# Reordering VectorE's masked products in the RWKV stage of a diffusion block kernel

## The reference

```python
def rwkv7_scan(r, w, k, v, kk, a, S):
    """All inputs (B,H,L,N); S (B,H,Nv,Nk).
    S_t = S_{t-1} (diag(w_t) - kk_t^T (a_t * kk_t)) + v_t^T k_t ;  y_t = S_t r_t."""
    def step(S, inp):
        rt, wt, kt, vt, kkt, at = inp
        sa = jnp.einsum("bhvk,bhk->bhv", S, -kkt)
        S = S * wt[:, :, None, :] + sa[..., None] * (kkt * at)[:, :, None, :] + vt[..., None] * kt[:, :, None, :]
        return S, jnp.einsum("bhvk,bhk->bhv", S, rt)
    S, ys = lax.scan(step, S, xs)
    return jnp.moveaxis(ys, 0, 2), S

y_c, y_l = bidir_scan(rwkv7_scan, init, *scan_args(pc), *scan_args(pl))
out_l = rwkv_out(y_l, pl, kvec, lnx, w_o)       # ((layernorm(y) + bonus) * g) @ w_o
```

## Time and profile before

| | |
|---|---|
| time before, median of 3 runs | 3686.1 us (3682.07 to 3688.07) |
| profiled execution, its own time | 3686.1 us |
| its span | 3684.3 us |
| TensorE busy (matmul) | 3408.9 us, 93% of the span |
| VectorE / ScalarE / GpSimd busy | 922.6 / 616.0 / 225.5 us |
| mean granted TensorE clock | 0.944 |
| HBM read | 567.19 MB |

### The profile page before, as it was taken

The page is one execution under the profiler, slowest core; times in us unless marked ns, Lnnn a source line. Parts: engine busy times, 40 slices in busy tenths (PEclk is TensorE's granted clock), DMA queues, the critical chain, the costliest instruction groups (busy, mean ns, idle before and its releaser), DMA issues. The chain is left out here.

```text
span 3684.3 us, 58147 instructions
## 1 busy us (share of the span) xinstructions
PE 3408.9 (93%) x25914; PEld 2490.3 (68%) x25914; DVE 922.6 (25%) x2050; ACT 616.0 (17%) x1416; POOL 225.5 (6%) x198
## 2 busy tenths in 40 slices
PE   6999996899999999999998799999989788888998
PEld 3777774698779877986456654444464577777887
DVE  0200015200001000101504514341030455553461
ACT  1010012200000000001313420000020334342100
POOL 0000000000000000000002210000000131311000
PEclk8999997899999999998998889999979999998999
DMA  9567741177777777775100113333321100003340
GB/s 376 225 249 305 309 175 58 52 286 274 282 281 284 276 282 283 282 276 212 57 35 2 59 68 117 123 114 145 118 83 40 40 23 13 23 3 139 117 158 23
DMA packets 86284, 577.28 MB, mean 157 GB/s; under 512 B 9488, under 2 KB 13584, under 8 KB 18192
## 3 DMA queue, kind: packets, MB, share of 16 engines
q1 hardware_dynamic: 82576, 568.27, 41.3%
q10 hardware_dynamic: 3456, 5.24, 0.4%
HBM read 567.19 MB, written 6.29 MB: 156 GB/s over the span
## 5 line engine op out<-in xcount | busy, mean ns | idle before, releaser
L261 PE MATMUL ps<-H,ring 128*128 128x256 f32 (+1 forms) x3600 | 1057.4, 456 | 16.8 <-ACT H L528 8.9
L261 PEld LDWEIGHTS ps<-H,ring 128*128 128x128 f32 x3600 | 693.9, 194 | 385.6 <-issue 317.8
L1399 PEld LDWEIGHTS ps<-W,ring 128*128 128x128 f32 x5632 | 639.5, 192 | 7.6 <-issue 3.3
L1399 PE MATMUL ps<-W,ring 128*128 128x128 f32 x5632 | 640.6, 275 | 1.2 <-ACT W L1432 1.2
L261 PE MATMUL ps<-W,ring 128*128 128x256 f32 (+1 forms) x1488 | 466.9, 475 | 10.4 <-DVE W L2514 8.0
L261 PEld LDWEIGHTS ps<-W,ring 128*128 128x128 f32 x1488 | 283.1, 191 | 197.7 <-issue 171.6
L1419 PE MATMUL ps<-ring,W 128*128 128x512 f32 x704 | 304.6, 592 | 0.0
L1480 DVE TENSOR_TENSOR W<-ps,W 128x128 f32<-128x128 f32 x176 | 51.3, 291 | 871.3 <-PE ps L1399 871.3
L1419 PEld LDWEIGHTS ps<-ring,W 128*128 128x128 f32 x704 | 132.6, 190 | 161.2 <-issue 161.2
L1648 DVE SCALAR_TENSOR_TENSOR W<-ps,vec,W 128x189 f32<-128x189 f32 (+3 forms) x396 | 173.3, 438 | 14.0
L3035 POOL TENSOR_TENSOR ring<-ring 128x512 f32<-128x512 f32 x96 | 124.5, 1313 | 528.3 <-DVE ring L3059 461.3
(11 more groups left out here) (386 smaller groups left out, 2692.8 us busy)
## 6 DMA issues: line engine op xcount, KB each, us to landing
ring<-weights SPq DMA_DIRECT2D x528, 1024.0 KB, 4.9
rkv<-W ACTq DMA_DIRECT2D x16, 256.0 KB, 2.0
ring<-rkv SPq DMA_DIRECT2D x8, 512.0 KB, 3.5
X<-tokens SPq DMA_DIRECT2D x1, 2048.0 KB, 8.1
ring<-rw_tiles SPq DMA_DIRECT2D x8, 256.0 KB, 3.8
const<-constants SPq DMA_DIRECT2D x1, 1168.0 KB, 10.5
rkv<-W ACTq DMA_DIRECT2D x8, 128.0 KB, 1.8
ring<-rkv SPq DMA_DIRECT2D x8, 128.0 KB, 3.6
```

What stands on the lines that cost most here:

```text
L261: mm = pe.matmul(out(o), lhsT=k.ring[:, k.slot(at), p * P:(p + 1) * P], rhs=rhs(kk), start=kk == 0, stop=kk == kt - 1)
L1399: mm = pe.matmul(ps[:, o % 4, 0:P], lhsT=w[:, i * P:(i + 1) * P], rhs=moe.Hg[:, kk, :], start=kk == 0, stop=kk == KD - 1)
```

## The change

VectorE's stream gets another order; nothing else is touched. `masked_grams` is dissolved. The masked products of both directions (L3059) now stand together behind the output work, the scaled `r` and `next_state(s, 2)`. The first matrix and its transpose are done for both directions, and only then `BKR` (L3136), which before stood between the two. All semaphores and their counts are the same.

```diff
--- before.py
+++ after.py
@@ -3053,12 +3053,6 @@
                     g = sc.G[s % 2][:, a:b + 1:b - a].unsqueeze(2).to_broadcast([P, 2, CH])
                     dve.tensor_tensor(sc.hat[(i + 1) % 2], ps[:, sc.U[0]:sc.U[1] + 1, 0:CH], g, ALU.mult).then_inc(sem["hat"], 1)
 
-            def masked_grams(j, z):
-                dve.wait_ge(sem["gram"], 2 * j + z + 1)
-                for h in range(2):
-                    dve.tensor_tensor(sc.LK[z][:, :, h], ps[:, ((0, 1), (2, 0))[z][h], :].rearrange("p (i b t) -> p i b t", i=2, t=CH),
-                                      sc.strict[z].unsqueeze(1).unsqueeze(1).to_broadcast([P, 2, 4, CH]), ALU.mult).then_inc(sem["lk"], 1)
-
             for j in range(TILES + 2):
                 s, q, prep = j - 1, j - 2, j < TILES
                 rkv = sc.rkv[j % 2]
@@ -3104,9 +3098,6 @@
                         dve.tensor_tensor(sc.bv[j % 3], ps[:, 2, S:2 * S], v_, ALU.mult).then_inc(sem["bv"], 1)
                         if q >= 0:
                             after(dve.scalar_tensor_tensor(sc.d, sc.d, sc.col(q, 6), ps[:, 2, 0:S], ALU.mult, ALU.mult))
-                if prep:
-                    masked_grams(j, 0)
-                next_state(s, 2)
                 if q >= 0:
                     if not prep:
                         dve.wait_ge(sem["rest"], j + 1)
@@ -3120,21 +3111,25 @@
                                                 r_.rearrange("p (c t) -> p c t", t=CH), sc.eR[z], ALU.mult)
                         ins.then_inc(sem["r"], 1) if z else ins.then_inc(sem["dve"], 1)
                     order[0] += 1
-                if prep:
-                    masked_grams(j, 1)
+                next_state(s, 2)
+                for z in range(2):
+                    if prep:
+                        dve.wait_ge(sem["gram"], 2 * j + z + 1)
+                        for h in range(2):
+                            out = sc.LK[z][:, :, h]
+                            dve.tensor_tensor(out, ps[:, ((0, 1), (2, 0))[z][h], :].rearrange("p (i b t) -> p i b t", i=2, t=CH),
+                                              sc.strict[z].unsqueeze(1).unsqueeze(1).to_broadcast([P, 2, 4, CH]), ALU.mult).then_inc(sem["lk"], 1)
                 next_state(s, 3)
                 if prep:
                     for z in range(2):
                         dve.wait_ge(sem["ot"], 12 * j + z + 1)
                         after(dve.tensor_tensor(sc.MT[j % 2][z], sc.OT[z][0], sc.unit.unsqueeze(1).to_broadcast([P, 8, CH]), ALU.add))
                         dve.transpose(flat(sc.M[z]), flat(sc.MT[j % 2][z])).then_inc(sem["m0"], 1)
-                        if z:
-                            break
-                        dve.wait_ge(sem["gram_r"], j + 1)
-                        for h in range(2):
-                            out = sc.BKR[j % 2][:, h].rearrange("p z i (b t) -> p z (i b) t", b=2)
-                            dve.tensor_tensor(out, ps[:, 1 + h, :].rearrange("p (z n t) -> p z n t", z=2, t=CH),
-                                              sc.upto.unsqueeze(2).to_broadcast([P, 2, 4, CH]), ALU.mult).then_inc(sem["bkr"], 1)
+                    dve.wait_ge(sem["gram_r"], j + 1)
+                    for h in range(2):
+                        out = sc.BKR[j % 2][:, h].rearrange("p z i (b t) -> p z (i b) t", b=2)
+                        dve.tensor_tensor(out, ps[:, 1 + h, :].rearrange("p (z n t) -> p z n t", z=2, t=CH),
+                                          sc.upto.unsqueeze(2).to_broadcast([P, 2, 4, CH]), ALU.mult).then_inc(sem["bkr"], 1)
                 next_state(s, 4)
                 for l in range(1, 6):
                     if prep:
```

## The result

The changed kernel takes 3714.5 us (median of 4 runs, 3712.6 to 3715.7), the kernel before 3685.4 in the same comparison: a ratio of 1.0079, 95% interval 1.0061 to 1.0097, some 29 us slower. The direction was forecast, the size was not: 3702.5 had been predicted, with a range up to 3712.

What follows compares the result with a forecast made beforehand. TensorE was taken to bound the kernel, busy 93% against VectorE's 25%. The terms -1.3 + 0.6 + 13.1 + 4 = +16.4 us, added to 3686.1, gave 3702.5 us, with a range of 3689 to 3712.

Steps and rivals of the forecast that it cites:

- Part 1: First masked product goes behind output work, both L3119 and L3054: -1.3 us together, and +0.6 us for tile 0.
- 1.16 at the full clock, I add 0.05: Second gram takes 1.16 us, plus 0.05 to VectorE's start: second L3059 at S+3.78 (S: start of first L3059 before).
- Part 2: Second L3129 and L3130 go in front of both L3136, which start 1.64 us later: 8 x 1.64 = +13.1 us.
- The hold-up by GpSimd: Second L3129 starts inside GpSimd's third product: L3136 is 1.64 us later, against 1.35 if GpSimd doesn't hold it up.
- The cover of 0.05: In tiles with twelve transposes in one piece, they hide only 0.05 us of L3136's delay, so these pay 1.6 too.
- The sum without its clock term: The order's own cost from moving the masked product and the first matrix: -1.3 + 0.6 + 13.1 us.
- The clock: Longer TensorE stops bring the low clock in all tiles; half a tile's 0.83 us in each: +4 us, an estimate.
- my upper bound of 13: Largest clock loss on TensorE: two losses of 0.83 us in each tile, 13 us.
- Rival B: No change: slack behind L2893, or earlier clock losses during L2883 disappearing, leaves +3 us, 3689; chance 0.12.
- Rival C: Faster: GpSimd's hold-up removed counts in full, the two L3059 back to back, part 2 hidden; -7 us, 3678; chance 0.07.
- the 1.03 of GpSimd's hold-up: L3114 takes 1.51 us beside GpSimd's product and 0.48 where GpSimd is idle; VectorE saves 1.03 us of busy time.

Runs made afterwards that it cites:

- part 1 with the stop filled: Kernel before with only the first masked product moved behind the output work, plus 8 unused matmuls before the second gram's wait: 3685.9 us, ratio 0.9998.
- +11 (1.0030, 1.0021 to 1.0039) with the stop filled: Kernel before with only the second first-matrix and transpose moved before BKR, plus 6 unused matmuls before the transposes that wait for BKR: 3700.4 us.
- part 2 alone: Kernel before with only the second first-matrix and its transpose moved in front of BKR: 3710.1 us, ratio 1.0069.
- the changed kernel with both stops filled: Changed kernel plus 8 unused matmuls before the second gram's wait and 6 before the transposes that wait for BKR: 3699.8 us, ratio 1.0032.
- the filled first stop alone: Changed kernel plus 8 unused matmuls in each tile, only before the wait of the second gram: 3713.7 us, ratio 1.0069.

## Why the prediction was wrong

*Part 1, -1.3 + 0.6 us.* The term holds at the full clock: part 1 with the stop filled measured 0.9998 (-1 us), and L2893 starts 0.2 sooner in tiles 2 to 7, as forecast. All its steps stand in the timeline of after: 0.48 for L3114, the gram 0.83 behind the masked product, the waits behind it absorbed. The addition "1.16 at the full clock, I add 0.05" was made in the wrong state, though: in the changed kernel the gram runs at the low clock in all tiles but tile 6, 1.98 in tile 3.

*Part 2, +13.1 us.* The term was right as well: +11 (1.0030, 1.0021 to 1.0039) with the stop filled, and BKR 1.69 later in tile 3. The hold-up by GpSimd was rightly counted for part 2 alone (the second L3129 takes 1.01) but not in the changed kernel itself, where in tiles 2 to 5 the first matrix is caught one product later, and the second goes free (0.65). The cover of 0.05 in the tiles with twelve transposes was read rightly too.

*The sum without its clock term*, +12.4, agrees with the changed kernel with both stops filled: ratio 1.0032, +12 us (8 to 16), of which up to 2.4 is the price of the matmuls in tiles 0 and 1.

*The clock, +4 us: the step that failed.* "I take half a tile's 0.83 in each" was a term of 4 us, and it measures 0.0047 of the time, 15 to 17 us (3714.5 against 3699.8; 1.0079 against 1.0032), with an interval of some 10 to 25 and up to 2.4 more for the price of the matmuls. That is beyond my upper bound of 13 by its middle, and not by its interval. Three things were wrong in it. I read rows 11 as a fall behind the stop itself. In tiles 1 and 3 to 5 the low stretch begins in the first gram instead, before the lengthened stop, and lasts through it and the second gram. I counted a low stretch as the loss of one gram, while it covers all dense work that follows: transposes, a state step, L2893. And I took the losses as hidden in part by the wait for BKR; in the changed kernel they aren't, since BKR itself waits for the first matrix, which waits for the state step that TensorE did slowly, and is then caught by one more GpSimd product (1.24 us in tiles 2 to 5 between the second masked product and the first transpose). By the middle of all three comparisons the bigger share (13 to 14 us) belongs to the stop in front of the transposes, and the smaller (4 to 6 us) to the one of 2.3 to 3.4 us in front of the second gram, though that is the longer; the intervals overlap. A reason would be that behind the shorter one no engine but TensorE sets the pace; that is argued from the order and wasn't tried.

*Rival B* expected that low stretches of before, during L2883, would go and give something back. They do go (in tile 4 the 62 matmuls of L2883 take 1.15 for 2.02), and nothing is given back: the kernel before with matmuls in its stop has lost them too, with L2893 no sooner and no change in time (1.0003). *Rival C* failed at the place that was named for it: the two masked products don't stand back to back, the second waits 1.59 for the gram. But the 1.03 of GpSimd's hold-up that it rested on was real, and worth more than forecast once the gram was left where it was.

*What stays open.* Where the clock falls differs between executions of one kernel, and a profile shows one of them, so the shares of the two stops are known from the ratios alone, whose intervals are wider than the smaller share. The profile of the changed kernel even puts most of its loss in tiles 2 to 5, at the first stop, and the filled first stop alone got little of it back, because the second stop then had its low stretch in every tile from 1 on. What decides whether the clock falls behind a given stop isn't shown. That the GpSimd product catches the first matrix was seen, and not tried by itself.

## What to carry to other kernels

Before an instruction is moved behind others, look at what the engine that waits for it does meanwhile: it is not only late, it may come back at half speed, or stay there. In this kernel the price of a stop in a dense TensorE stream was its length plus what the low stretch behind it cost, up to 1.2 us in a tile at the second stop and up to 1.7 at the first, where a GpSimd product came on top, and nothing where VectorE set the pace. Where VectorE and GpSimd both read SBUF, find the VectorE instructions that take longer than the same line elsewhere, and move GpSimd's start by its semaphore rather than VectorE's order.

## What the runs showed of the hardware

- TensorE's clock fell behind stops of 1.7 us (tile 4 before) to 2.7 us (part 2 alone, tile 6), not only behind the one of 3.4 us. The length of one stop doesn't settle it: the clock stayed at 1.00 behind one of 1.21 us (part 2 alone, tile 5), of 1.71 us (tile 3 before) and of 2.18 us (tile 3 of the changed kernel).
- Once low, it stayed low through a further stop: at 0.50 from the first gram to the transposes in tile 3 of the changed kernel, some 10 us, where with matmuls in that stop the second gram ran at the full speed again (1.16).
- Matmuls that compute nothing made a kernel faster: 14 of them in each of eight tiles took the changed kernel from 3714.5 to 3699.8 us.
- A float32 matmul of 128x128 on 128 columns shows as two matmul instructions, and 24 of them took 6.07 us in a piece that began at the low clock.
- A VectorE instruction with two SBUF operands that meets running GpSimd products looks as if it gets its turn between two of them: it ended 0.55 us after the one it met (L3126 in the changed kernel, 128x512) or 0.27 us after (L3114, 128x256), and four GpSimd products in a row then took 5.43, where one alone takes 1.27.
